# Clearing a stage's semaphores inside the next stage, and a later wait for the identity

## The reference

```python
def reference(x, w_in, ..., final_norm_w_3):
    x = first_block(x, w_in, lb_logits, hg_norm_w, sinks, w_out, ln_g, ln_b)
    x = second_block(x, norm_g_2, w_in_2, ..., w_out_2, final_g_2)
    return third_block(x, norm_w_3, w_in_3, ..., w_out_3, final_norm_w_3)
```

## The kernel before

| stage | function | work |
|---|---|---|
| hg | `hgrn` | first block, recurrence |
| sw | `window_attention` | first block, attention, output projection |
| rp | `rwkv_project` | second block, projection for the recurrence |
| rw | `rwkv` | second block, recurrence |
| fp | `fox_project` | second block, projection for the attention |
| fa | `forgetting_attention` | second block, attention |
| po | `project_block` | second block, output projection |
| sh | `short_mixers` | third block, projection and short mixers |
| rc | `recurrences` | third block, projection and recurrences |
| pl | `project_block` | third block, output projection |

## Time and profile before

### The profile page before, as it was taken

How to read it: one execution, slowest core, us unless ns; L and a number is a source line. 1 busy time by engine, 2 the same in 40 slices (tenths; PEclk the granted TensorE clock), 3 DMA queues, 4 the chain that set the end, 5 groups by cost and what they waited for, 6 DMA issues and landing times. The chain is left out here.

```text
span 4864.5 us, 68578 instructions
## 1 busy us (share of the span) xinstructions
PE 4324.6 (89%) x25175; PEld 3600.8 (74%) x25232; DVE 2582.0 (53%) x5011; ACT 1319.1 (27%) x2626; POOL 598.9 (12%) x585
## 2 busy tenths in 40 slices
PE   8999788888599986999997997899979799799879
PEld 6777577777477766888886886777768677677667
DVE  4344434344366665777764334777743443576733
ACT  3222212222222221111112113666631211222211
POOL 0000011111100002333331110000000011011100
PEclk9999899999799998999998998999989999999989
DMA  3111311111333332111122324310033423322233
GB/s 129 55 60 60 126 45 59 58 58 59 137 122 132 129 116 69 47 45 37 38 98 83 113 108 144 122 36 18 10 115 132 148 104 129 124 86 92 93 116 116
DMA packets 218307, 434.14 MB, mean 89 GB/s; under 512 B 36419, under 2 KB 90436, under 8 KB 218022
## 3 DMA queue, kind: packets, MB, share of 16 engines
q1 hardware_dynamic: 218150, 432.08, 25.9%
HBM read 248.40 MB, written 146.93 MB: 81 GB/s over the span
## 5 line engine op out<-in xcount | busy, mean ns | idle before, releaser
L236 PE MATMUL rp_pj<-rp_w_high,rp_hT_high 128*128 128x512 f32 (+1 forms) x640 | 239.9, 384 | 26.9 <-DVE rp_w_low L228 14.1
L236 PE MATMUL fp_pj<-fp_w_high,fp_hT_high 128*128 128x512 f32 (+2 forms) x640 | 220.1, 358 | 31.1 <-DMA fp_ident<-const_ident 21.8
L2518 DVE TENSOR_SCALAR_CACHE_REDUCE fa_sm<-fa_sc 128x512 f32<-128x512 f32 (+2 forms) x320 | 194.3, 609 | 92.6 <-PE fa_sc L2359 81.1
L237 PE MATMUL rp_pj<-rp_w_low,rp_hT_high 128*128 128x512 f32 (+1 forms) x640 | 234.1, 375 | 0.0
L236 PE MATMUL hg_pj<-hg_w_high,hg_hT_high 128*128 128x512 f32 x512 | 211.0, 412 | 15.7 <-DVE hg_w_low L228 15.7
L237 PE MATMUL fp_pj<-fp_ahead_w_low,fp_hT_high 128*128 128x512 f32 (+2 forms) x640 | 217.4, 354 | 0.0
L236 PE MATMUL rc_pj<-rc_w_high,rc_hT_high 128*128 128x512 f32 (+1 forms) x512 | 191.7, 382 | 23.3 <-DMA rc_ident<-const_ident 12.6
L237 PE MATMUL hg_pj<-hg_w_low,hg_hT_high 128*128 128x512 f32 x512 | 206.1, 403 | 0.0
L2373 PE MATMUL fa_tp<-fa_ident,fa_sm 128*128 128x128 f32 x1088 | 175.1, 282 | 31.3 <-DVE fa_pT_low L178 14.6
L2466 ACT CAST fa_pT_high<-fa_tp 128x512 fp32r<-128x512 f32 (+1 forms) x288 | 161.1, 560 | 147.2 <-PE fa_tp L2373 144.9
L178 DVE TENSOR_TENSOR fa_pT_low<-fa_tp,fa_pT_high 128x512 fp32r<-128x512 f32 (+1 forms) x288 | 188.8, 656 | 13.2 <-ACT fa_pT_high L2466 12.9
(11 more groups left out here) (560 smaller groups left out, 11264.6 us busy)
## 6 DMA issues: line engine op xcount, KB each, us to landing
rw_given<-rw_packed_dram SPq DMA_DIRECT2D x48, 512.0 KB, 4.1
rc_back<-rc_XB SPq DMA_DIRECT2D x48, 336.0 KB
rw_packed_dram<-rp_M SPq DMA_DIRECT2D x48, 256.0 KB, 2.6
rp_M<-rp_U SPq DMA_DIRECT2D x16, 728.0 KB, 4.7
hg_xt<-in_x SPq DMA_DIRECT2D x16, 512.0 KB, 3.9
kept_x_high_dram<-hg_hT_high SPq DMA_DIRECT2D x16, 512.0 KB, 3.6
kept_x_low_dram<-hg_hT_low SPq DMA_DIRECT2D x16, 512.0 KB, 4.4
sw_hT_high<-kept_x_high_dram SPq DMA_DIRECT2D x16, 512.0 KB, 3.6
```

The lines of the kernel that those rows point to most:

```text
L236: pe.matmul(out, hT.high[:, kc, :], high[:, kc, lo:hi], start=kc == 0, stop=False)
L237: pe.matmul(out, hT.high[:, kc, :], low[:, kc, lo:hi], start=False, stop=False)
L2518: dve.tensor_scalar(sm[:, to:to + cols], bank_of(slot)[:, 0:cols], 0.0, NEG, ALU.add, ALU.max, accum_out=tops[:, four, c:c + 1]).then_inc( ...
```

## The change

The clearing block between two stages is gone. A stage's semaphores are no longer given back, nor cleared, when its function is left. They stay held (`held`), and the stage is put on a list (`Stage.left`). In the next stage's block SP clears them (`clear_left`) behind its first loads. When that next stage is left in its turn, the semaphores cleared in it are given back. Since the numbers stay taken for a stage longer, a few waits of the later stages use other semaphore numbers than before. The last stage's semaphores are cleared in a block of their own as before, by `Stage(nc, None, "end").clear()`. A consumer of `Raw` weights now names the stage that loaded them (`join`) in place of adding its semaphores to its own list. In fp, PE's wait for the identity moves from the head of its stream to the transposes of tile 0.

```diff
 class Stage:
+    left = []
     def __init__(self, nc, ctx, name):
-        self.nc, self.ctx, self.name, self.sems = nc, ctx, name, []
+        self.nc, self.ctx, self.name, self.sems, self.held = nc, ctx, name, [], ExitStack()
+        self.joined = []
...
     def sem(self, name):
-        self.sems.append(self.ctx.enter_context(self.nc.semaphore(f"{self.name}_{name}")))
+        self.sems.append(self.held.enter_context(self.nc.semaphore(f"{self.name}_{name}")))
         return self.sems[-1]
+    def join(self, other):
+        self.joined.append(other)
     def block(self):
-        self.ctx.callback(self.clear)
+        self.ctx.callback(self.leave)
         return self.ctx.enter_context(self.nc.Block())
+    def clear_left(self, sp):
+        for stage in Stage.left:
+            for one in stage.sems:
+                sp.sem_clear(one)
+    def leave(self):
+        self.release()
+        Stage.left = [self, *self.joined]
+    def release(self):
+        for stage in Stage.left:
+            stage.held.close()
+        Stage.left = []
     def clear(self):
         with self.nc.Block() as block:
             @block.sync
             def _(sp):
-                for one in self.sems:
-                    sp.sem_clear(one)
+                self.clear_left(sp)
+        self.release()
...
@@ in SP's stream of sw, rp, rw, fp, po and pl, sh, rc
+            s.clear_left(sp)
             pipeline(sp, step)
...
@@ fox_project
         def _(pe):
-            pe.wait_ge(ident_here, 16)
-
...
                     need(pe, kT_ready, 2 * t)
+                    if isinstance(t, int) and t == 0:
+                        pe.wait_ge(ident_here, 16)
                     for c in range(4):
                         pe.transpose(tq[:, c * P:(c + 1) * P], qk[pt][:, c * P:(c + 1) * P], ident[:])
...
@@ build_program, at its end
+    Stage(nc, None, "end").clear()
```

More of the change, by code:

```diff
@@ L187, in __init__ @@
     def __init__(self, s, name, n, quarters):
+        self.stage = s
         with s.nc.sbuf_tensor(f"{s.name}_{name}_loaded", [P, KC, n], F32) as loaded:
@@ L207, in __init__ @@
         for one in raw:
-            s.sems += one.here
+            s.join(one.stage)
         widths = [hi - lo for lo, hi in cols]
```

## The result

| | before | after |
|---|---|---|
| median | 4871.72 us (4 runs) | 4838.45 us (4 runs) |
| lowest to highest | 4864.82 to 4877.98 | 4835.69 to 4850.24 |
| the profiled execution, its own time | 4866.29 | 4850.24 |
| its span | 4864.5 | 4848.4 |

The changed kernel takes 0.9937 of the time of the kernel before (95% interval 0.9917 to 0.9958). From the medians that is 33 us less, from the ratio 31, where 27 were forecast; 4838 lies within the forecast range of 4832 to 4863. Most of this part goes into where its other 11 us are.

A forecast was written before the change was run, and what follows sets the result against it. PE, busy 4324.6 of 4864.5 us, was taken to bound the kernel, with the clearing stretches serial for the whole core. 28.3 - 0 - 1 + 0 = 27 us off gave a forecast of 4846 us, range 4832 to 4863.

The forecast's parts named there:

- What leaves the path: Between stages: nine clearing blocks, serial for the whole core, go; 25.1 us of clears plus nine times 0.35, 28.3 us.
- The barrier's share: At nine transitions: what a clearing block costs besides its clears, 0.35 us each, 3.2 us in all.
- The clears on SP's queue: In each next stage: 428 clears delay SP's later issues by 1.4 to 3.6 us, covered by holdups and waits; cost 0.
- rival 2: Clears on SP's queue are on the path: 25.1 us return, 3.2 us gain left, 4869; chance 0.10.
- the only known danger: In fa, ACT waits for second queries loaded behind the clears: cost 0, with no cover 3.2 us.
- The identity: In fp, moving PE's wait for the identity gains 0, bounds 0 and 0.2 us; the second chunk's start stays.
- What is late next: At stage starts: first work moves up with the one barrier, except for code fetches and TensorE's clock; 1 us taken off.
- The fetch of code: At nine stage starts: a hole of 0.6 us each would cost 5.4 us, none 0; 1 us taken.
- Rival 1: Holes of 0.6 us at nine starts, clears sticking out in fa and rp by 3.2 and 0.6: gain 19 us, 4853; chance 0.10.
- The clock: TensorE at 1.2 GHz at stage starts: starts move against its rises, 0 taken, 5 us allowed each way.
- The prediction's own alarm: Sign of being wrong: a stage between two starts longer than before by more than a microsecond.
- Rival 3: In rw's loop, PE's short idles drop the clock in more tiles: slower, 4888; chance 0.03.

The follow-up runs named there:

- b_ranges: Kernel before, clearing blocks kept, neighbouring semaphore numbers cleared by one instruction, 21 clears instead of 428 between stages: 4843.06 us, ratio 0.9950.
- b_double: Kernel before, every semaphore cleared twice in the clearing blocks: 4894.82 us, ratio 1.0060.
- a_ident_first: Kernel after, with PE's wait for the identity put back to the head of its stream in fp: 4841.57 us, ratio 0.9946.
- a_first: Kernel after, with the clears ahead of each stage's first load instead of behind the loads: 4863.21 us, ratio 0.9989.
- a_ranges: Kernel after, with neighbouring semaphore numbers cleared by one instruction, in the stages and in the end block: 4837.51 us, ratio 0.9936.
- a_four: Kernel after, every semaphore cleared four times in its place: 4857.16 us, ratio 0.9976.
- before_again: Kernel before, unchanged, profiled once more: 4866.79 us, one execution.
- b_ident_late: Kernel before, with only PE's wait for the identity in fp moved to the transposes: 4876.95 us, one execution.
- a_again: Kernel after, unchanged, run once more: 4841.33 us, ratio 0.9952.

## Why the prediction was right

**What leaves the path.** The step held: nine stretches of clears are serial time. The kernel after gives it up (0.9937), b_ranges gives it up with the blocks left in place (0.9950), and b_double pays it a second time (1.0060). 28.3 us were worked out; with the clock taken out the two profiles of the kernel after show 27.1 and 23.2 and a_ident_first 22.7, so 1 to 6 us less, and b_ranges 22.4 of the 25 us of clears that it saves. Where the rest stays was not found, but for a part in fa (below). The barrier's share of 3.2 us is not settled by itself: a_first measures 6 us with an interval from 1 to 10, and b_ranges, which keeps the barriers, can't be told from the kernel after.

**The clears on SP's queue.** Cost 0 was the choice, and rival 2, all of them on the path, the alternative. Rival 2 fell: SP's holdups shrank from 6.13, 3.54, 4.81 and 2.54 us by about the time of the clears, and a_ranges, with hardly any clears, is not faster by more than the noise. a_four shows how far the cover reaches: over 60 of 75 us more. The term that was set too low is fa's, the one that the prediction itself had called the only known danger. ACT's wait for the second queries is 5.27 and 5.38 us in the two profiles of the kernel after, 4.74 and 4.17 in those of before, and its cast comes 27.9 and 27.8 us after fa's start instead of 27.5 and 27.0. So 0.3 to 0.9 us of 3.2 are paid there; a_ranges, at 4.83 us and 27.4, may get some of it back. A third profile with the same code in fa, that of a_ident_first, is worse: the cast comes at 30.1 us.

```profile
2991.57 0.62 ACT L2457 CAST fa_qT_high<-fa_q_loaded 128x512 fp32r<-128x512 f32 x1 [5.87 <-DMA fa_q_loaded<-queries_dram]
```

There 1.4 us were lost ahead of the clears, at a load of queries on which SP sat for 3.53 us instead of 2.15. That leaves up to 1.7 us for the clears. The reason given was wrong in form: that the queries land as late as before because the DMA engines never run dry would hold for a_four too, where they landed 9.5 us later. That rw's clears fit into SP's wait holds, but by way of five loads that go out later and are not missed.

**The identity.** As worked out: the releaser is now `hT_low`, the chunk behind stays at its place, and the value is 0. A figure was off. The idle time before the second chunk was to be 1.1 us; it is 1.75 in the kernel after and between 0.6 and 1.8 in the others, wherever the wait stands: DVE fixes the start of the second chunk, and the figure is what the first chunk happens to leave of the time before it.

**What is late next.** The fetch of code was put at 1 us of a possible 5.4. Nothing of it can be seen on the path: ACT's first cast in sw stands 0.1 us behind the barrier, and SP's first load 0.07 to 0.09 at all nine starts, as before. The Trainium skill, "Runtime: NRT & Kernel Launch", section "Instruction fetch mechanics", has an engine stall for a fetch at a taken branch that leaves the fetched window. The rows of sw's and po's starts have no room for such a stall on the path (po's first transpose moved by 2.27 of 2.35 us); whether the branches there leave the fetched window no run shows. The holes that remain stand in the clears, where SP has time, and go with a fetch, by the packets behind them (b_double). Their size was overstated: of hg's 0.6 us one gap is 0.42 over the pitch, and the rest is a pitch of 58 ns instead of 55, so that nine of them would be under 4 us and not 5.4. Rival 1 asked for them at the starts, and fell with that; of its other part, fa's 3.2 us, less than a third came in two profiles and at most half in the third.

**The clock.** The 5 us allowed each way are too few for one execution: the kernel after lost 11 us to it in rw and got 7 back in sw, and its two profiles are 35 us apart in their time at 1.2 GHz, 250.6 and 215.6, worth 17.5 us. The prediction's own alarm, a stage longer by over a microsecond, went off in rw, and it was this. For medians the step was good enough. Rival 3's mechanism is real, but nothing shows that the change sets it off: rw's 5292 matmuls took PE 660.6, 663.1 and 668.7 us in three profiles that keep the old clears (before, before_again, b_ident_late) and 671.1 and 660.4 in two of the kernel after.

**The time.** 4846 was the forecast and 4838 the median. The sum was 27 us and 31 are measured (0.9937, between 20 and 40), and 23 for a_again (0.9952); the sum lies between. The agreement is no closer than that noise. The base of 4871.9 against the 4871.72 measured beside the kernel after says little, since three of those four runs are the ones that the forecast was made from; of the 8 us 6 are the sum's and the rest is rounding up. In the other batches, of 11 and 21 runs, the median of before is 4864.65 and 4869.41, so a time by itself is good to some 5 us here, a ratio to 0.2%. The upper end of the range, 4863, does not come out of the terms given for it either: 4878 - 19 is 4859. Nothing hangs on it here.

**A version that beats both** was not found: a_ranges, the one that had to be tried, is at 0.9936, as the kernel after. It is worth knowing that b_ranges gets three quarters of the gain or more (0.9950 against 0.9937 and 0.9952) by one helper, with no stage's order touched.

## What to carry to other kernels

Look up by line what a profile does not count as busy, clears and barriers above all, and ask of each stretch whether any engine has work beside it: here 428 instructions of 25 ns, 55 ns apart, were 25 us in which the whole core stood still. Then reduce their number first (one instruction for a range of semaphores), and move what is left to a place where its queue is held up anyway, behind the first loads and not ahead of them, which cost 22 us here. Before explaining why one profile shows only half of the gain, compare PE's busy time for equal counts of matmuls, stage by stage.

## What the runs showed of the hardware

- One clear of a range of 53 semaphores took 118 ns (b_ranges); 53 single ones take 3.0 to 3.6 us. The price is by the instruction, some 55 ns on SP, far more than by the semaphore.
- Clears keep their pitch beside busy DMA engines: 52 took 3.2 us in an otherwise idle core and 3.3 us in fa's head, where the DMA share in the window from 2985 to 3003 us is 1.05.
- A row of SP's clears is broken now and then by one gap of 0.4 us, followed 0.6 to 0.9 us later by one instruction packet of 8 KB (nine of nine in b_double, four of four in the kernel before; 0.8 to 3.7 us later in the kernel after, beside running DMAs).
- SP was held at some issues for 2.5 to 6.1 us, where the shortest take 0.33 to 0.43. Clears ahead of such an issue shortened the holdup by about their own time, and cost the stage nothing or little.
- One program's matmuls of one stage are granted 1.2 GHz for 49 us in one execution and for 72 in another (rw of the kernel after, in a_again and in the first profile), with no difference in its order or its work. What decides it was not found.
